# First stage: the index chain ahead of the weight splits; end: half the tokens scaled and stored early

## The reference

```python
# layer 1, mixer A: attention over 128 keys that an indexer selects for each query
q, k, v, iq, ik, iw, z = split(h @ w_in)        # 16 heads of q, one k and v, 16 index heads of 64
iq, ik = rotary(iq), rotary(ik)
rel   = relu(einsum('bqhd,bsd->bqsh', iq, ik))
score = einsum('bqsh,bqh->bqs', rel, iw)        # causal, then the 128 largest of each row
o = attention of q over the selected k, v
y = (o * silu(z)) @ w_out
# layer 2, mixer B: banded, dilated attention of 16 heads, same gate and output projection
# end
out = h * rsqrt(mean(h * h, -1) + 1e-6) * final_g
```

## Time and profile before

| what | us |
|---|---|
| median of three runs | 941.82 |
| the profiled execution | 942.12 |
| its span, first to last instruction | 940.2 |
| TensorE busy (share of the span) | 927.3 (99%) |
| weight loads of TensorE | 804.0 (86%) |
| VectorE busy | 596.3 (63%) |
| ScalarE busy | 425.0 (45%) |
| GpSimd busy | 554.8 (59%) |

### The profile page before, as it was taken

One profiled execution on the slowest core, in us unless ns is written; L12 is line 12 of the kernel. 1 busy time (PEld: TensorE's weight loads), 2 busy tenths in 40 slices (PEclk: granted clock), 3 DMA queues, 4 the chain that ended last, 5 costly groups with the idle time before them and its releaser, 6 DMA issues.

```text
span 940.2 us, 13251 instructions
## 1 busy us (share of the span) xinstructions
PE 927.3 (99%) x4863; PEld 804.0 (86%) x4863; DVE 596.3 (63%) x1245; ACT 425.0 (45%) x773; POOL 554.8 (59%) x424
## 2 busy tenths in 40 slices
PE   9899999999999999999999999999999999999996
PEld 8798888888888888888888898989898888988886
DVE  6899798666656641136766666666767666665226
ACT  6674422455445543253443445452534434453323
POOL 2774544555555544457666677666766667764535
PEclk9999999999999999999999999999999999999998
DMA  9321323111211123221222222222222222132312
GB/s 341 124 90 68 112 90 111 47 46 45 68 46 45 46 90 113 90 90 66 70 90 90 89 72 68 87 90 89 70 72 85 90 90 90 56 102 89 113 45 90
DMA packets 25265, 81.48 MB, mean 87 GB/s; under 512 B 2928, under 2 KB 5232, under 8 KB 25200
## 3 DMA queue, kind: packets, MB, share of 16 engines
q1 hardware_dynamic: 24048, 79.57, 25.6%
q10 hardware_dynamic: 1152, 1.06, 0.3%
HBM read 78.52 MB, written 2.10 MB: 86 GB/s over the span
## 4 chain that ended last, share of the span: by engine, by line
PE 94%; DVE 3%; POOL 2%; issue 1%; ACT 0%; POOLq 0%; DVEq 0%; ACTq 0%
PE ps L350 16%; PE ps L351 16%; PE ps L352 16%; PE ps L483 6%; PE ps L482 6%; PE ps L484 6%; PE ps L385 3%; PE ps L384 3%; PE ps L383 3%; PE ps L431 2%; PE ps L432 2%; PE ps L433 2%; PE ps L446 2%; PE ps L474 1%; PE ps L473 1%; PE ps L463 1%
## 5 line engine op out<-in xcount | busy, mean ns | idle before, releaser
L1363 POOL TENSOR_TENSOR w_lo<-w_raw,w_hi 128x1024 fp32r<-128x1024 f32 x136 | 328.8, 2424 | 181.9 <-ACT w_hi L691 181.1
L350 PE MATMUL ps<-u_hi,w_hi 128*128 128x512 f32 (+1 forms) x712 | 276.0, 388 | 0.8 <-DVE rotated L1068 0.7
L351 PE MATMUL ps<-u_lo,w_hi 128*128 128x512 f32 (+1 forms) x712 | 274.6, 386 | 0.0
L352 PE MATMUL ps<-u_hi,w_lo 128*128 128x512 f32 (+1 forms) x712 | 274.6, 386 | 0.0
L350 PEld LDWEIGHTS ps<-u_hi,w_hi 128*128 128x128 f32 x712 | 134.0, 188 | 27.2 <-DVE rotated L1068 0.9
L351 PEld LDWEIGHTS ps<-u_lo,w_hi 128*128 128x128 f32 x712 | 133.9, 188 | 25.7 <-issue 0.2
L352 PEld LDWEIGHTS ps<-u_hi,w_lo 128*128 128x128 f32 x712 | 133.8, 188 | 25.6
L691 ACT ACTIVATE w_hi<-w_raw 128x1024 fp32r<-128x1024 f32 x136 | 141.7, 1054 | 25.5 <-DMA w_raw<-weights 15.2
L1143 DVE STREAM_TRANSPOSE bias_a<-neg_s 32x320 f32<-32x320 f32 x240 | 120.7, 503 | 25.2 <-POOL neg_s L1414 22.2
L783 ACT ACTIVATE probs<-neg_s,neg_max 128x128 f32<-128x128 f32 (+3 forms) x128 | 70.7, 553 | 47.3 <-DVE neg_max L1125 47.3
L1424 POOL TENSOR_TENSOR pT_lo<-bias_a,pT_hi 128x896 fp32r<-128x896 f32 (+1 forms) x30 | 46.6, 1574 | 70.5 <-ACT pT_hi L797 70.5
(11 more groups left out here) (180 smaller groups left out, 1762.9 us busy)
## 6 DMA issues: line engine op xcount, KB each, us to landing
w_raw<-weights SPq DMA_DIRECT2D x136, 512.0 KB, 3.3
gated<-x_rows SPq DMA_DIRECT2D x4, 512.0 KB, 8.3
h<-x_turned SPq DMA_DIRECT2D x7, 256.0 KB, 5.7
outT<-h SPq DMA_DIRECT2D x10, 128.0 KB, 1.9
w_raw<-weights SPq DMA_DIRECT2D x4, 256.0 KB, 4.8
table<-rope_tables SPq DMA_DIRECT2D x2, 512.0 KB, 7.2
outT<-h ACTq DMA_DIRECT2D x6, 128.0 KB, 2.2
neg_s<-weights SPq DMA_DIRECT2D x1, 512.0 KB, 6.7
```

The source lines that it names most:

```text
L350: pe.matmul(out, w_hi[:, g % SLOTS, blk], u_hi[:, k, tokens], start=(at == 0), stop=False)
L351: pe.matmul(out, w_hi[:, g % SLOTS, blk], u_lo[:, k, tokens], start=False, stop=False)
L352: last = pe.matmul(out, w_lo[:, g % SLOTS, blk], u_hi[:, k, tokens], start=False, stop=(at == KT - 1))
L1363: pool.tensor_tensor(w_lo[:, g % SLOTS, :], w_raw[:, g % 2, :], w_hi[:, g % SLOTS, :].bitcast(F32), ALU.subtract).then_inc(w_lo_ready, 1)
```

## The change

In the first stage:

- GpSimd copies the causal mask before the key's low parts (the mask gets a semaphore of its own), then makes the low parts of index query 0, and only then splits tile 6; index_lo(1), split 7, index_lo(2), split 8 follow, each split one place later than before. ScalarE splits tile 8 behind relu(0) and index_hi(2) instead of ahead of them.
- VectorE scales gate 0 ahead of index_rope(1). For t from 1 on, index_rope writes the cosine product back into its PSUM bank and the sum reads it there; the sum, no longer the product, frees the bank. The key rope keeps the old form under a new name.
- ScalarE's queue issues x block 0 ahead of the gains.

At the end:

- Three heads instead of two run in halves (`ENDING`).
- The first half's sum goes behind block 1 of the second half, its spread behind block 3; VectorE scales blocks of the first half between the residual additions of the second. All eight are scaled by VectorE and stored on both queues.
- Of the second half, ScalarE multiplies by the gain, TensorE turns the blocks back to rows (16 transposes into banks 3, 4, 6, 7), and ScalarE and VectorE scale rows by the reciprocal root while reading PSUM, 512 wide, two each. They are stored as four parts of 256 KB. The output is two tensors, one turned (1024 x 256) and one of rows (256 x 1024).
- GpSimd adds up seven squares instead of six in the second half, and scales nothing.

```diff
-POOL_OUT, DVE_OUT = (2, 4, 6), (0, 1, 3, 5, 7)
-POOL_SQUARES = 6
+ENDING = 3
+POOL_SQUARES = 7
+ACT_STORES = {0: 3, 2: 5, 4: 7, 6: KT}
+ROW_BANKS = {(2, 0): 3, (2, 1): 4, (3, 0): 6, (3, 1): 7}
+ACT_ROWS, DVE_ROWS = ((2, 0), (3, 0)), ((2, 1), (3, 1))
...
@@ tensor
-                for at in range(added, KT + 1):
+                pe.wait_ge(last_added, half * (KT - 1) + added - 1)
+                for at in range(added - 1, KT):
...
+            def turn_rows(blocks):
+                for at in blocks:
+                    m = M_ORDER[at]
+                    pe.wait_ge(rows_gained, at + 1)
+                    for i in (2, 3):
+                        bank = ROW_BANKS[i, m // 4]
+                        pe.wait_ge(residual_ready, 3 * KT + M_ORDER.index(bank) + 1)
+                        last = pe.transpose(ps[:, bank, m % 4 * P:(m % 4 + 1) * P],
+                                            gained[at][:, (i - 2) * P:(i - 1) * P], ident[:, :])
+                last.then_inc(rows_turned, 1)
...
+                heads = range(HEADS - (ENDING if layer else 2), HEADS)
...
-                    if layer and at == 4:
+                    if layer and ends and at == 1:
                         sum_last_squares(0)
+                    if layer and ends and at == 3:
+                        spread_first_half()
...
-            spread_last(0)
+            turn_rows(range(0, 5))
             sum_last_squares(1)
-            spread_last(1)
+            turn_rows(range(5, KT))
@@ scalar
+                    if half:
+                        act.activation(gained[at], h[:, m, tokens], ACT.Copy, scale=scale).then_inc(rows_gained, 1)
+                    if half and at == 1:
                         last_root(0)
...
+                    for stored, behind in ACT_STORES.items():
+                        if half and behind == at:
+                            store_first(stored)
...
+            def last_rows():
+                store_first(6)
+                act.wait_ge(inv_turned_ready, 4)
+                for i, f in ACT_ROWS:
+                    act.wait_ge(rows_turned, f + 1)
+                    act.activation(out_parts[i, f], ps[:, ROW_BANKS[i, f], :], ACT.Copy,
+                                   scale=inv_turned[:, i:i + 1]).then_inc(act_rows_ready, 1)
...
+            act.dma_start(h[:, 0, :], xT[0:P, :]).then_inc(x_landed[0], 16)
             act.dma_start(gain[:, :], gains).then_inc(gain_landed, 16)
-            act.dma_start(h[:, 0, :], xT[0:P, :]).then_inc(x_landed[0], 16)
...
-            split_w(G_V + AHEAD)
             relu(0)
             index_hi(2)
+            split_w(G_V + AHEAD)
@@ vector
+            def last_rows():
+                dve.wait_ge(inv_turned_ready, 4)
+                for i, f in DVE_ROWS:
+                    dve.wait_ge(rows_turned, f + 1)
+                    dve.tensor_scalar(out_parts[i, f], ps[:, ROW_BANKS[i, f], :], inv_turned[:, i:i + 1], None,
+                                      ALU.mult).then_inc(dve_rows_ready, 1)
...
@@ index_rope(t)
-                index_products(G_IQ[t], CHOOSING, 4)
+                    sin = dve.tensor_tensor(by_sin[out, CHOOSING], ps[other, BANK[n], CHOOSING],
+                                            table[other, 3, CHOOSING], ALU.mult)
+                dve.wait_ge(sin_ready, 2 * t)
+                dve.tensor_tensor(ps[:, BANK[n], CHOOSING], ps[:, BANK[n], CHOOSING], table[:, 2, CHOOSING],
+                                  ALU.mult).then_inc(cos_ready, 1)
+                dve.wait_ge(cos_ready, t)
                 if r >= 2:
                     dve.wait_ge(rope_lo_ready, r - 1)
-                dve.tensor_tensor(rotated[:, r % 2, CHOOSING], by_cos[:, CHOOSING], by_sin[:, CHOOSING],
-                                  ALU.add).then_inc(rotated_ready, 1)
+                dve.tensor_tensor(rotated[:, r % 2, CHOOSING], ps[:, BANK[n], CHOOSING], by_sin[:, CHOOSING],
+                                  ALU.add).then_inc(bank_read[BANK[n]], 1)
...
+            scale_gate(0, G_Z[0])
             index_rope(1)
-            scale_gate(0, G_Z[0])
...
-            for at in range(KT - 1):
-                last_residual(1, at)
-            last_inverse(0)
-            last_residual(1, KT - 1)
-            last_copy(0)
...
+            for at in range(KT):
+                if at == 2:
+                    last_inverse(0)
+                    dve.wait_ge(inv_turned_ready, 3)
+                    diagonal(range(QB // 2))
+                last_residual(1, at)
+                if at == 3:
+                    dve.wait_ge(spread_done, 3)
+                if 3 <= at < KT - 1:
+                    last_scale(at - 3)
+            for at in range(KT - 4, KT):
+                last_scale(at)
             last_inverse(1)
+            last_rows()
@@ gpsimd
+            pool.wait_ge(causal_landed, 16)
+            for i in range(1, QB):
+                last = pool.tensor_copy(score[:, OFF[i] - P + i * P:OFF[i] + i * P], bias_a[:, 0:P])
+            last.then_inc(score_zeroed, 1)
...
-            split_w(6, moved=R_IQ)
-            index_lo(0, 6)
...
-            split_w(G_Z[0] + AHEAD)
-            index_lo(1, G_Z[0] + AHEAD)
-            split_w(G_V + AHEAD, moved=R_IQ + 2)
-            index_lo(2, G_V + AHEAD)
+            index_lo(0, 5)
+            split_w(6, moved=R_IQ + 1)
+            index_lo(1, 6)
+            split_w(G_Z[0] + AHEAD, moved=R_IQ + 2)
+            index_lo(2, G_Z[0] + AHEAD)
+            split_w(G_V + AHEAD, moved=R_IQ + 3)
```

More of the change, by code:

```diff
@@ L173, in build @@
         ordered = neg_s
+        gained = [table[:, at // 2, at % 2 * SEQ // 2:(at % 2 + 1) * SEQ // 2] for at in range(KT)]
+        out_parts = {(2, 0): by_cos[:, :], (3, 0): by_sin[:, :], (2, 1): rotated[:, 0, :], (3, 1): rotated[:, 1, :]}
         gain = sb("gain", [P, 3 * KT])
@@ L231, in rotated_at @@
         def rotated_at(r):
[L233 to L234 removed]
+            if r <= R_IQ or r in (R_K, R_B):
+                return rotated_ready, {R_K: R_IQ + 2, R_B: R_IQ + 3}.get(r, r + 1)
             of = (r - R_B) // 2 * 4 + (r - R_B) % 2
[L236 removed]
+            n = n_of(G_IQ[r - R_IQ] if r < R_K else G_Q[r - R_Q] if r < R_B else G_B + of)
             return bank_read[BANK[n]], TURN[n] + 1
@@ L497, in out_projection @@
                         pe.wait_ge(gated_ready, HEADS)
-                    end = layer == 1 and t == HEADS - 3
+                    end = layer == 1 and t == HEADS - ENDING - 1
                     last = out_block(layer, t, m, ALL, t == 0, end)
@@ L510, in last_out_projections @@
                         pe.wait_ge(residual_ready, (2 if ends else 1) * KT + at + 1)
-                    last = out_block(layer, HEADS - 2, m, tokens, layer == 1, False)
-                    if ends and m == M_ORDER[-1]:
-                        last.then_inc(tile_done, 1)
-                    last = out_block(layer, HEADS - 1, m, tokens, False, True)
-                    if ends and m == M_ORDER[-1]:
-                        last.then_inc(tile_done, 1)
-                    else:
-                        last.then_inc(y_done, 1)
-                    if not ends:
-                        continue
-                    if layer and at == 4:
+                    for t in heads:
+                        if layer and not ends and at == 0:
+                            wait_for_head(1, t)
+                        last = out_block(layer, t, m, tokens, layer == 1 and t == heads[0], t == HEADS - 1)
+                        if ends and m == M_ORDER[-1]:
+                            last.then_inc(tile_done, 1)
+                        elif t == HEADS - 1:
+                            last.then_inc(y_done, 1)
+                    if layer and ends and at == 1:
                         sum_last_squares(0)
+                    if layer and ends and at == 3:
+                        spread_first_half()
             def head_a(hd):
@@ L948, in _ @@
             last_root(1)
-            for half in range(2):
-                for at in POOL_OUT:
-                    m, tokens = M_ORDER[at], HALVES[half]
-                    act.wait_ge(out_pool, half * len(POOL_OUT) + POOL_OUT.index(at) + 1)
-                    act.dma_start(outT[m * P:(m + 1) * P, tokens], h[:, m, tokens]).then_inc(out_stored, 16)
+            last_rows()
         @block.vector
@@ L1052, in scale_first, with key_rope @@
                                   ALU.mult).then_inc(rotated_ready, ready)
+            def key_rope():
+                n, half = n_of(G_K), P // 2
+                dve.wait_ge(tile_done, G_K + 1)
+                dve.wait_ge(*rotated_at(R_K - 1))
+                for out, other in ((slice(0, half), slice(half, P)), (slice(half, P), slice(0, half))):
+                    dve.tensor_tensor(by_sin[out, :], ps[other, BANK[n], :], scaled[other, 1, :], ALU.mult)
+                dve.tensor_tensor(by_cos[:, :], ps[:, BANK[n], :], scaled[:, 0, :], ALU.mult).then_inc(
+                    bank_read[BANK[n]], 1)
```

(15 more changed lines are left out.)

119 lines of the change are left out of this document (57 added, 62 removed).

## The result

The changed kernel takes 937.40 us (median of 6 runs, 937.08 to 937.72); the kernel before, in the same rounds, 942.18 (940.94 to 944.36). The ratio is 0.995, interval 0.9939 to 0.9961: faster by about 0.5%, and inside the forecast of 937.1 (935.4 to 939.6). Of the kernel before, later rounds gave medians of 942.5 to 942.6 over 9 to 17 runs; the 941.82 that I started from was on the low side by 0.4 to 0.8. It depends on the share of quick runs among them: of 40 later runs 8 took 940.7 to 941.2 us, all with a mean granted clock of 0.997, and the other 32 took 942.1 to 944.0, all but one with 0.992 to 0.996. The profiled execution took 937.72 with a span of 935.9, against 940.2: 4.3 us less.

What follows compares the result with a forecast made beforehand. TensorE, holding 94% of the chain of waits, was taken to bound the kernel, with VectorE the bound from 47.90 to 92 us. Terms 0.2 + 3.3 + 1.2 = 4.7 us off the 941.82 median gave 937.1, range 935.4 to 939.6.

Steps and rivals of the forecast that it cites:

- GpSimd's order: First stage: mask copies and query 0's low parts ahead of tile 6's split let VectorE take G_IQ[3] 4.0 us earlier.
- The index sum: VectorE's index rope: the sum, reading PSUM, loses no more time for t=1 to 3; 1.43 us for t=3.
- Tile 9 takes its place: First stage: ScalarE's split of weight tile 9 ahead of relu(1) becomes the limit, leaving 3.3 us gain (3.0 to 3.7).
- Key rope: Near 92 us, where TensorE waits 0.7 us: key_rope is the rope that stood there, with no gain of its own.
- Input order: Start: x block 0 issued one place earlier on ScalarE's queue gives 0.2 us, bounds 0 and 0.44.
- The end: Last projection and the scalings and stores behind it: the span closes 1.2 us earlier, bounds 0.2 and 2.2.
- Rival 1: Tail: transposes and four large stores merely replace the sixteen small ones, giving nothing; 938.3 us, chance 0.16.
- rival 2: First stage gives back more, by low clock or later relu(1): 1.0 to 1.7 of 3.3 us remain; 939.4, chance 0.10.
- rival 5: First stage: index scores wait for something else and still start near 39.8; 940.4 us, chance 0.06.
- rival 4: Landing times: slow loads of weight tiles 8 to 10 and slow last stores; 944.3 us, chance 0.03.
- Rival 3: First stage and end: tile 9 is no bound and the stores take only their latency; 935.3 us, chance 0.05.

Runs made afterwards that it cites:

- relu first: The changed kernel with ScalarE's relu(1) ahead of its split of weight tile 9: 934.67 us, ratio to the kernel before 0.9917; run again, 934.82.
- end-alone run: The changed kernel with its first stage put back as before the change and only the new end kept: 940.11 us, ratio to the kernel before 0.9976.
- two heads: The changed kernel with two heads instead of three in halves at the end (ENDING = 2): 939.27 us.
- GpSimd's old order: The changed kernel with GpSimd's mask copies and tile 6 split, and ScalarE's tile 8 split, in their old places, new rope forms kept: 938.07 us.

## Why the prediction came out right, step by step

**GpSimd's order: right.** TensorE's first index scores start at 38.27; less the 1.24 us by which the key copy of this profile is later (32.17 for 30.93) that is 37.03, and 37.0 was forecast. TensorE's own work was only 0.50 us later in this profile, and its stand of 0.54 comes from that difference; in the second one, with the key copy at 31.46, the scores start at 37.57 without a stand. VectorE takes G_IQ[3] at 45.28, or 44.04 by the same reckoning (forecast 43.9, before 47.90). The clock stayed at 1.00. The stand for tile 6's low part is 0.18 (forecast 0.3).

**The index sum: right in size, wrong in its reach.** The sum takes 0.56 where it took 1.99. I let it count for t=3 alone, but in the new order t=4 would have been hit as well. The Trainium skill (SBUF — State Buffer, "SBUF: two separate sides") has the rule of the exclusive lock, and this case's traces agree, with 2.05 and 2.42 us for a sum of 0.56. They agree at the key's rstd product as well. I had looked only at the mask copies behind it, and there it came as said: they take 1.22 us instead of 0.76 and the loss falls into idle time. What I had not seen is the split of tile 5 ahead of both. The product took 1.79 us at 30.35 beside that split, which ran from 29.20 to 31.60, and 1.05 before the change; this wait is where stage one begins.

**Tile 9 takes its place: right, and shown by relu first, though its gain was taken too high.** The split starts at 49.67 less 1.24 = 48.43, the additions 19.08 us behind the key copy instead of 21.75: 2.7 us, where 3.3 was taken and 3.0 to 3.7 allowed. The load landed in 4.3 us, just past the 4.2 that I had as its slow end, and the first relu hands over 0.6 us after its start (50.64 to 51.25), not 0.4.

**Key rope: wrong, as the step said it.** "key_rope is the rope that stood there" is false, and so is the sentence on it in the section on the change. The old one multiplied in place and freed its bank with the sum; the new one writes by_cos in SBUF and frees the bank 0.7 us earlier, which ends the wait that I had quoted myself. That is worth 0.7 us by the wait and 1.0 by its experiment. It fills what tile 9 left missing: 2.7 of tile 9's place, less 0.2 (from the additions for t=1 to those for t=6 it is 33.42 us instead of 33.21, most steps 6.65 for the forecast's 6.60), and 0.7 make 3.2. The profiled pair has 2.04 and the 1.24 by which it began later, 3.28; the medians, start included, have 3.05. So stage one came near the forecast's 3.3 + 0.2, but out of other parts. That is luck: the two steps that missed, tile 9 and the key rope, missed in opposite directions.

**Input order: wrong.** +0.2 was the sum's term; the experiment shows no gain that stands out of the scatter. I looked only at who waited for x and not at what comes behind 256 KB in the same queue.

**The end: the right mechanism, its size too small.** 1.2 us forecast, 2.3 to 2.4 measured, slightly beyond the upper bound of 2.2. This is the term of the sum that was most wrongly sized. Before, the last issue (937.2) lay 25.15 us behind the mark and the span ended 3.0 behind it; now it is 22.44 and 3.45. So the issue came 2.71 earlier and 0.45 is given back: 2.26. The forecast had 22.9 and 4.0. Of the first miss, 0.22 had arisen when the last matmul ended (18.13 behind the mark for 18.35: the spread did not stand, and the diagonal took 0.48 and not 0.95). The second is in the bytes of the stores: at 320 GB/s I had them end 3.15 us behind the last issue, and they ended 2.6 behind it (935.05); at that point they ran at 383 GB/s, where the stores of before had 343. The 0.85 us from there to the end of the span were right. Why the bytes ran faster stays open: it isn't the second queue, and it isn't that no other engine works by then, for the 343 of before were without one too. The larger pieces (2 KB for 1 KB) and the fewer, larger transfers are left; no run here parts them.

On the rule of the Trainium skill that issuing engines are not separate queues (DMA: Bandwidth & Descriptors) the runs agree, with 0.3 us between two queues and one. The same page gives its fit for DMAs issued from GpSimd, and I applied it to stores issued from SyncE and ScalarE. It came out at 2.6 us for the last landing, which took 3.1; the first of the four, at 2.1, was below it. That the later ones are slower because all four are under way together is likely and not shown.

**The rivals.** Rival 1 (no gain at the end) is refuted by the end-alone run, rival 2 by the clock, the 0.18 us and stage one's 3 us, rival 5 by the scores at 38.27. Nothing of rival 4 came: tile 9's load took 3.4 to 4.8 us in the runs, and 7.2 was its point. Rival 3 was nearer about the end's gain (2.0), though the last landing was more than a latency, and wrong about tile 9.

**The parts do not add.** GpSimd's order, the sum and the key rope, each taken out alone, cost 1.0 + 1.6 + 1.0 = 3.6 us, and all of them together 3.05 (by the table 1.2 + 1.7 + 0.7 = 3.6, and 3.3).

**The total: partly luck.** In the rounds of the experiments the change is worth 942.48 - 937.06 = 5.4 us, not 4.7. That the time itself came out at 937.1 owes as much to the 941.82 that I started from, 0.7 below those rounds, as to the sum.

## What to carry to other kernels

When a stall is removed, follow every consumer on to the next in-order queue and ask what stands ahead of its work there: here one 1 us split that waits 4.2 us for a load stood ahead of a 0.4 us relu, and swapping them gave 2.4 us, beside 3.05 for the whole edit of stage one. Price such an edit also with the next delay gone, since one delay hides another (1.6 against 3.0 us for the same sum). Compare the old and new forms of every helper by what releases its buffers, not by its arithmetic. And see that an experiment has reached what it is to change: the packet count of a profile tells at once that a store was not cut into smaller pieces.

## What the runs showed of the hardware that I had not expected

A VectorE product of two SBUF operands, 64x512, begun beside a GpSimd weight split, took up to 2.08 us where the shortest of 14 took 0.68, and what followed it started 0.57 to 0.60 us after the split's end in all 14 traces. GpSimd loses as well: the first of three mask copies that begin while that product runs took 0.75 us and the others 0.29.

TensorE stood 0.54, 0.58, 0.81 (two heads) and, in the kernel before, 0.7 us with its clock at 1.00; a stand of 1.39 us near the end was followed by 3.3 us at the lower level, 1.2 GHz (granted 0.58 in the mean from 926.0 to 928.5). The 2.54 us stand of the earlier trace rows lies in a stretch of 0.84. A stand of this length does not seem to cost the clock every time: GpSimd's old order, whose trace has it, took 936.3 and 936.8 us at a mean of 0.999, and 937.9 to 939.6 at 0.996 to 0.997. Only one of its executions has a trace, so this is read from the means.

A 12 KB load issued behind a 256 KB one on the same queue landed in 4.1 to 4.4 us in eleven traces, and in 3.1 to 3.3 in the three in which it went first. The 512 KB load of tile 9 took 3.4 us in two traces and 4.1 to 4.8 in the others, although the median of its kind is 3.3; why it is mostly longer at that place was not found.

With all 16 DMA engines busy, stores in 1 KB pieces ran at 343 GB/s and stores in 2 KB pieces, fewer and larger, at 383; from one queue they ran as fast (385).
